# Hybrid decoder step: page scores moved from VectorE to TensorE, and all page loads issued by SyncE

## The reference

```python
past_kv = (gather_pages(kv[0], i, kv[2]), gather_pages(kv[1], i, kv[2]))
z = einsum('bthd,bshd->bhts', q, k) * DH_A ** -0.5 + bias_h      # one score per head and position
u = where(causal, log_sigmoid(-z), 0)
after = cumsum(u, reverse=True) - u                              # from the last position back
w = where(causal, exp(log_sigmoid(z) + after), 0)
o = einsum('bhts,bshd->bthd', w, v)
```

## Time and profile before

| | us |
|---|---|
| median of 3 runs | 4942.42 (4940.56 to 4952.39) |
| profiled execution | 4942.47 |
| its span | 4940.5 |
| `pb_phase` in it (us from the start) | 237 to 455 |
| `attention_phase` | 455 to 717 |
| `rwkv_phase` | 717 to 1911 |

### The profile page before, as it was taken

The page is one execution under the profiler, slowest core; times in us unless marked ns, Lnnn a source line. Parts: engine busy times, 40 slices in busy tenths (PEclk is TensorE's granted clock), DMA queues, the critical chain, the costliest instruction groups (busy, mean ns, idle before and its releaser), DMA issues. The chain is left out here.

```text
span 4940.5 us, 82596 instructions
## 1 busy us (share of the span) xinstructions
PE 4001.3 (81%) x29517; PEld 3331.4 (67%) x29517; DVE 2583.9 (52%) x3393; ACT 1226.2 (25%) x1915; POOL 238.8 (5%) x302
## 2 busy tenths in 40 slices
PE   6786877666667775699999968995878876999998
PEld 6685333333333335699999968894777766999998
DVE  2156878777788834334443434444675423443443
ACT  3212551122211121222223322222222212222232
POOL 0000000000000000000000000000011000000000
PEclk8898998877778887899999989996778888999999
DMA  2243017766778752211115422222012031111244
GB/s 93 74 151 120 26 48 261 251 222 224 226 239 274 246 147 77 90 51 43 52 52 159 154 85 85 87 82 79 24 44 78 19 137 75 46 43 51 75 157 135
DMA packets 284216, 566.08 MB, mean 115 GB/s; under 512 B 37185, under 2 KB 103105, under 8 KB 277418
## 3 DMA queue, kind: packets, MB, share of 16 engines
q1 hardware_dynamic: 177946, 375.32, 23.8%
q10 hardware_dynamic: 90000, 141.65, 8.8%
q0 software_dynamic: 16032, 45.92, 2.3%
HBM read 504.38 MB, written 58.79 MB: 114 GB/s over the span
## 5 line engine op out<-in xcount | busy, mean ns | idle before, releaser
L261 PE MATMUL ps<-ffn_hh,up_wh 128*128 128x344 f32 x2112 | 677.6, 321 | 59.5 <-DVE up_wl L253 59.5
L263 PE MATMUL ps<-ffn_hl,up_wh 128*128 128x344 f32 x2112 | 675.9, 320 | 0.0
L262 PE MATMUL ps<-ffn_hh,up_wl 128*128 128x344 f32 x2112 | 675.1, 320 | 0.0
L1052 PE MATMUL ps<-pg_v,pg_w 128*8 128x512 f32 x1024 | 382.8, 721 | 155.6 <-DMA pg_v<-in_v_pages 104.0
L261 PEld LDWEIGHTS ps<-ffn_hh,up_wh 128*128 128x128 f32 x2112 | 397.9, 188 | 60.6 <-issue 60.6
L263 PEld LDWEIGHTS ps<-ffn_hl,up_wh 128*128 128x128 f32 x2112 | 397.9, 188 | 0.0
L262 PEld LDWEIGHTS ps<-ffn_hh,up_wl 128*128 128x128 f32 x2112 | 397.8, 188 | 0.0
L457 PE MATMUL ps<-down_ah,down_wh 128*128 128x344 f32 x1056 | 346.1, 328 | 53.0 <-DVE down_al L489 31.7
L1113 DVE TENSOR_TENSOR pg_prod<-pg_k,pg_q 128x1024 f32<-128x1024 f32 x256 | 316.3, 1236 | 47.6 <-DVE rw_mxt L1424 13.5
L459 PE MATMUL ps<-down_al,down_wh 128*128 128x344 f32 x1056 | 339.8, 322 | 0.0
L458 PE MATMUL ps<-down_ah,down_wl 128*128 128x344 f32 x1056 | 339.5, 321 | 0.0
(11 more groups left out here) (430 smaller groups left out, 7367.3 us busy)
## 6 DMA issues: line engine op xcount, KB each, us to landing
pg_k<-in_k_pages SPq DMA_DIRECT2D x512, 256.0 KB, 4.3
pg_v<-in_v_pages ACTq DMA_DIRECT2D x512, 256.0 KB, 4.5
down_w<-in_w_down SPq DMA_DIRECT2D x96, 704.0 KB, 4.1
up_w<-in_w_ff SPq DMA_DIRECT2D x44, 1034.0 KB, 4.8
odd_w<-in_w_odd SPq DMA_DIRECT2D x33, 526.0 KB, 4.1
scratch_odd_rows<-odd_cv POOLq DMA_DIRECT2D x32, 516.0 KB, 4.6
dn_x<-scratch_odd_rows SPq DMA_DIRECT2D x8, 1536.0 KB, 7.8
scratch_x<-out_x POOLq DMA_DIRECT2D x16, 516.0 KB, 3.0
```

The source lines that it names most:

```text
L261: pe.matmul(out, wh, xh, start=(k == 0), stop=False)
L262: pe.matmul(out, wl, xh, start=False, stop=False)
L263: mm = pe.matmul(out, wh, xl, start=False, stop=(k == n - 1))
L1052: pe.matmul(self.T.ps[c:c + H_A, 7, :], wts[:, :, g], self.vp[:, n, :], start=(g < 4), stop=(g >= NPG - 4), tile_position=(0, c), skip_gro ...
```

## The change

K pages are now stored transposed in memory (512 columns as four blocks of 128 partitions, positions along the row), still 256 KB each with 2 KB per partition. PE forms scores of 8 pages at once (a round, `keys_pe`): 16 matmuls with the query of one sample as a 128x32 stationary operand and 256 positions moving, in the four column groups. ACT copies the result out of PSUM (`scores_act`), PE transposes it back (`turn_pe`), and DVE adds the bias (`bias_dve`, 64 elements per partition). The products and sums on DVE go away. A sample has 8 rounds.

V pages are waited for and used in groups of four (16 groups for a sample). All page loads are issued by SP, a V group and a K round in turn, in an order fixed in the new `pair` of SP: V group 0, 1, 2, 3, K round 0, V 4, V 5, K round 1, and so on to V 13, K 5, V 14, K 6, V 15, K 7. The K ring holds two rounds (16 pages), the V ring two groups (8 pages). Some tiles of `rwkv_phase` now share memory to make room. In `pb_phase` the loops of SP, PE, ACT and DVE are written out.

```diff
+    def page(self, sp, g):
+        return bass.ds(sp.value_load(self.table[0:1, bass.ds(g, 1)], min_val=0, max_val=self.T.n_phys - 1), 1)
+    def load_keys(self, sp, b, r):
+        at = NPG * b + self.ROUND * r
+        sp.wait_ge(self.k_used, at + self.ROUND)
+        for n in range(self.ROUND):
+            slot = self.ROUND * (r % 2) + n
+            sp.dma_start(self.kp[:, slot, :, :], self.T.io["k_pages"][self.page(sp, at + n), :, :, :]
+                         .rearrange("a p c t -> (a p) c t")).then_inc(self.k_in[r % 2], 16)
+    def load_values(self, sp, b, q):
+        at = NPG * b + self.GROUP * q
+        sp.wait_ge(self.v_used, at + self.GROUP)
...
+    def keys_pe(self, pe, b, r):
...
+        pe.wait_ge(self.k_in[r % 2], 512 * b + 128 * (r // 2) + 128)
+        alone(pe, self.passed)
+        first = self.ROUND * (r % 2)
+        for c in range(4):
+            for j in range(4):
+                mm = pe.matmul(self.T.ps[32 * j:32 * j + 32, 6, 0:2 * PAGE], self.qb[:, c, :],
+                               self.kp[:, first + j:first + self.ROUND:4, c, :], start=(c == 0), stop=(c == 3),
+                               tile_position=(0, 32 * j), skip_group_check=True)
+        mm.then_inc(self.k_used, self.ROUND)
+    def scores_act(self, act, b, r):
+        act.wait_ge(self.k_used, self.RING + NPG * b + self.ROUND * (r + 1))
+        act.activation(self.zt[:, :], self.T.ps[:, 6, 0:2 * P], ACT.Copy).then_inc(self.z_copied, 1)
...
         @block.sync
-            with sp.Fori(1, NS) as b:
-                pages.load_keys(sp, b)
+            def pair(i, keys=True):
+                for q in range(16):
+                    pages.load_values(sp, i, q)
+                    r = (q - 3) // 2 if q < 14 else q - 8
+                    if keys and q >= 3 and (q % 2 or q >= 14):
+                        pages.load_keys(sp, i + 1, r)
+            with sp.Fori(0, LAST) as i:
+                pair(i)
+            pair(LAST, keys=False)
...
         def _(pe):
+                def between(n):
+                    more(1)
+                    if n % 2:
+                        score(n // 2 + 1)
+                    else:
+                        turn(n // 2)
...
                     mm.then_inc(S["mixed"], 1)
-                    more(4)
+                    turn(5 + p)
+                    more(1)
+                    score(6 + p)
                 finish_pe(pe, i, o[:, :, :], W)
+                turn(7)
                 pages.select_pe(pe, i)
...
         def _(act):
-                asked = iter(range(4, NPG))
-                def fetch(to):
-                    for g in asked:
-                        pages.load_values(act, i, g)
...
         def _(dve):
-                units = iter(range(0, NPG, 2))
-                def more(n):
-                    for _, g in zip(range(n if keys else 0), units):
-                        pages.keys_dve(dve, i + 1, g // Pages.RING, g % Pages.RING)
+                bias = lambda r: pages.bias_dve(dve, i + 1, r) if keys else None
...
-    L["k_pages"] = A["cache_k"][0].reshape(-1, PAGE, D_A)
+    L["k_pages"] = A["cache_k"][0].reshape(-1, PAGE, 4, P).transpose(0, 3, 2, 1)
```

More of the change, by code:

```diff
@@ L870, in _ @@
             weights(0, 1)
-            pages.start_sp(sp)
-            keys(0)
-            with sp.Fori(1, NB_T // 2) as i:
+            sp.wait_ge(pages.table_in, 16)
+            pages.load_keys(sp, 0, 0)
+            for i in range(1, NB_T // 2):
                 weights(i, 0)
-                keys(i)
+                pages.load_keys(sp, 0, i)
                 weights(i, 1)
-            keys(NB_T // 2)
+            pages.load_keys(sp, 0, NB_T // 2)
         @block.tensor
@@ L881, in _ @@
             pages.start_pe(pe)
-            with pe.Fori(0, NB_T // 2) as i:
+            for i in range(NB_T // 2):
                 for j in range(2):
@@ L905, in _ @@
             round_weights(act, wh[:, 0, :], w[:, 0, 0:KT * P], w_rounded)
-            with act.Fori(0, LAST) as i:
+            pages.start_act(act)
+            for i in range(LAST + 1):
                 tile(i, 0)
-                tile(i, 1)
-            tile(LAST, 0)
-            tile(LAST, 1, True)
+                pages.scores_act(act, 0, i)
+                tile(i, 1, i == LAST)
+            pages.scores_act(act, 0, LAST + 1)
         @block.vector
@@ L1015, in load_key_page @@
[L1015 to L1028, removed]
@@ L1560, in prep_act @@
             act.sem_inc(S["k_rn"], 1)
-            if sample is not None:
-                fetch(12)
             act.wait_ge(S["l_ready"], i + 1)
@@ L1577, in prep_dve @@
             tt = lambda o, a, b, op: dve.tensor_tensor(o, a, b, op)
-            if sample is not None:
-                pages.bias_dve(dve, sample)
-                dve.wait_ge(pages.biased, sample + 1)
             dve.wait_ge(S["w_exp"], i + 1)
@@ L1705, in pair @@
                 gram(4, t["B"], Rx)
-                more(4)
-                solve_levels_pe(pe, T, S, i, mtl, xm, xt, y, (5, 2, 1), S["pe_passed"], lambda: more(4))
+                more(1)
+                score(0)
+                slots = iter(range(10))
+                solve_levels_pe(pe, T, S, i, mtl, xm, xt, y, (5, 2, 1), S["pe_passed"], lambda: between(next(slots)))
                 pe.wait_ge(S["masked"], i + 1)
@@ L1755, in _ @@
                 pair(i)
-            pair(LAST)
+            pair(LAST, keys=False)
             i = NPAIR
```

213 lines of the change are left out of this document (101 added, 112 removed).

## The result

The changed kernel takes 5154.6 us (median of 4 runs, 5145.5 to 5159.1) beside 4947.4 us (median of 4) for the kernel before on the same chip: ratio 1.042, 95% interval 1.040 to 1.044. It is 4.2% slower. One of the four runs of the kernel before took 12532 us, for which the record has no cause; the other three lie between 4940.6 and 4952.4 us with the median at 4942.4, against which the ratio is 1.043. The forecast was 5165 us, range 5090 to 5240.

What follows compares the result with a forecast made beforehand. It took SyncE's stream of page issues, with a stop inside each pair, to bound the changed kernel: 4942.5 + 248 - 3 - 21 = 5166 us, rounded to 5165. The range for 8 times in 10 was 5090 to 5240 us.

Steps and rivals of the forecast that it cites:

- The case that was given the highest chance: Whole kernel: SyncE's page stream with one long stop a pair makes it slower, 5165 us; chance 0.72.
- The page as the deciding term: SyncE's stream in `rwkv_phase`: issuing one page costs 1.17 us (1.13 to 1.24), so 128 pages take 150 us a pair.
- The ring: Period of a pair in `rwkv_phase`: 120 page issues, landing, scores, normalisation, weights, first V group; 180.3 us, before 144.9.
- The stop: SyncE stands still near 29 us a pair before V group 2, which waits until group 0 has been used.
- VectorE's relief worth nothing in `rwkv_phase`: Freeing VectorE of 78.7 us a pair gains nothing there, since the page stream is what waits.
- `rwkv_phase`: Seven pairs with keys were to cost +248 us, the last pair without keys -3 us.
- `pb_phase`: VectorE's page units leave the ring and PE becomes the bound: -21 us (-26 to -5), next phase beginning near 434 us.
- Later phases: `attention_phase` and all phases after it were taken as unchanged: 0 us.
- The first, one queue that keeps up: Issue cost hidden: the last pair's 108 us and eight rounds of 2.6 us, 129 us a pair; 4807 us; chance 0.05.
- The second, a stream that never stands still: SyncE's wait for group 0 is covered: 152 us a pair, +25 us, 4967 us; chance 0.08.
- The third, several stops: SyncE's stream held up more than once a pair: 10 to 12 us a pair more, 5240 to 5250 us; chance 0.13.

Runs made afterwards that it cites:

- 0.91 us a page: Changed kernel with one table read per page kept but the bound test behind it taken away: 4928.9 us, ratio 0.999 to the kernel before.
- 0.6 and 0.526: Changed kernel with a round's or group's page numbers read at once, without bound test: 4774.6 us; changed kernel with the table not read: 4776.7 us.
- The sums on VectorE: Changed kernel with unused sums over constants added on VectorE, four a tile of `pb_phase` and eight a level of the solve: 5181.7 us in one run.
- the early K rounds: Changed kernel with K rounds 0 and 1 of the next sample issued ahead of V group 2 in SyncE's stream: 5046.9 us, ratio 1.019.
- cheap reads: Page numbers read eight (K) or four (V) at once, without bound test: ratio 0.968 in the changed kernel, 0.993 in the kernel before.
- all three moves together: Changed kernel with cheap reads, the early K rounds and the normalisation and select ahead of round 7's scores: 4760.8 us, ratio 0.965.
- the third move: Normalisation and select put ahead of K round 7's scores: alone on the changed kernel 5099.1 us; added to the other two moves 4760.8 us, without it 4742.2.

## Why the prediction was right

The case that was given the highest chance came about, at 5154.6 instead of 5165 us.

- **The page as the deciding term.** 1.17 us was taken; the median is 1.166, the mean over the ring's 120 pages 1.21 (now and then a DMA instruction takes 0.62 us instead of 0.33). 0.91 us a page gives 149.7 us a pair; 0.6 and 0.526 give 128.2 and 126.3, where SyncE has to wait for PE in other places too. The Trainium skill's rule (DMA: Bandwidth & Descriptors, "Issuing engines are not separate DMA queues") that issuing is usually small beside the DMA itself doesn't hold here: with the same data and queue, cheaper issuing alone took the kernel from 1.042 to 0.968 of the one before.
- **The ring.** 180.3 forecast, 179.9 measured, and the factor of 120 pages measured as 117. Its terms were less good than their sum. The 120 pages took 144 us (from V group 2 at 1081.6 us to the last K page at 1225.8), not 142. The chain from the last page's issue at 1045.9 back to V group 2 took 35.8 us, not 38.3. Landing took 3.0 us instead of 4.3; the 4.3 had been read from the kernel before, where ScalarE issued V pages beside SyncE, and with V pages on ScalarE again it is 4.7. The score took 3.64 instead of 3, at a granted clock of 0.50. From L1638 to the next opening it was 5.9 instead of 11, since ScalarE, which issues no V pages there now, opens the pair beside the normalisation. From the opening to the weights it was 19.7 instead of 17.3, for the bias then stands behind the normalisation on VectorE. From the weights to SyncE's next issue it was 3.6 instead of 2.7. The errors cancel, partly by luck.
- **The stop.** Near 29 us was forecast as one. From issue to issue the trace has 22.5 to 24.7 us before V group 2 and 4.2 to 4.8 us at the loop's turn, each with a page's own 1.17 us in it: 25 to 27 us of standing still in all. The second lies inside the chain above and costs nothing. Its place and its cause, V group 2 waiting for group 0's use, were right.
- **VectorE's relief worth nothing in `rwkv_phase`.** Shown: 46 us of idle work a pair move nothing.
- **`rwkv_phase`.** +248 - 3 = +245 forecast, 1436.9 - 1194.8 = +242 measured.
- **`pb_phase`.** -21 forecast, -24 measured: it ends at 430.5 us, 434 forecast. The sums on VectorE gave 9 us back, so the direction of the reason is shown, not its parts.
- **Later phases.** Taken as 0. The profile has -16 in the delta phase, of which the second profile of the kernel before shows at least 12 to be chance; in the profiled run, 5145.5 us, that is most of the 20 us to 5165.
- **The rivals.** The first, one queue that keeps up, was turned down because a page would have to cost less than 0.74 us. Runs on both sides agree with that threshold: at 0.91 us a page the ring still sets the pair, and with a page near 0.6 us the pair is 128.2 us (129 forecast) and the kernel 4775 us (4807 forecast, 11 of the 32 us between are that the kernel before took 4931.6 beside it, not 4942.5). That 129 was hit so closely is luck, as its last pair was 11 us too long and its price of the keys 11 us too low. The second, a stream that never stands still, would be 152 us a pair; the early K rounds removed the stop and reached only 164, with 1.21 us a page and 9 us of short pauses. The third, several stops, didn't occur.

Among the experiments, three theories failed. For the V pages on ScalarE, I counted that queue's issue time as free and it was not. For the early K rounds on top of cheap reads, I took SyncE's ring to be out of the pair and it was not. For all three moves together, the time fell below the theory's range too, though the third move itself cost time.

## What to carry to other kernels

Before work is moved onto one queue, count what each of its issues costs in the sequencer, reads of tables and tests included, and multiply by all that stands in the ring; a stream at 1.17 us for 256 KB can be the bound while the data path idles. Look at an issue's parts before moving it: the cure was to read eight numbers with one instruction and without the test. Neither step was worth much by itself: cheap reads alone gave 0.7%, relieving the engine that looked busiest alone cost 4.2%, and both together gave 3.2%. The test is a safety that is then missing; whoever drops it has to know that the table holds valid numbers. And a reordering that helps under one bound (the normalisation first, 6.7 us a pair) can cost once the bound has moved.

## What the runs showed of the hardware

- One TENSOR_LOAD reads several numbers into registers: 0.27 us for one, 0.30 for four, about 0.52 for eight.
- The bound test of a page number, with one small register operation beside it, costs 0.258 us at the median, about as much as the read.
- From SyncE's backward branch to its next instruction pass 0.24 us in the kernel before, where the loop's body has 66 instructions; with bodies of 410 to 922 instructions it is 2.7 to 5.7 us, not in order of length (about 3.2 us at 922, 5.3 at 458). What sets it was not tested.
- K pages land after 3.0 us (median) when one queue issues pages 1.17 us apart, after 3.3 us at 0.91 us apart, and after 4.7 us when bursts are 0.52 us apart or when ScalarE issues V pages beside SyncE's.
